# Attention's second heads scaled by ScalarE, dense products spread anew over its steps, one signal per silu

## The chip, the cores and the metric

The kernel runs on one core of a Trainium2 chip. The metric is device microseconds of one execution; runs are compared by their medians. Before the change the median of 3 runs is 1513.92 us (1513.66 to 1514.63). TensorE is called PE here, VectorE DVE, ScalarE ACT, SyncE SP and GpSimd POOL.

## The reference

Two blocks follow each other on a sequence of 512 tokens of width 1024. Only part of the first block is touched. Its mixer has an SSM half and an attention half, each gated by a silu, and ends in a product with `w_out`:

```python
y_ssm = s5_mixer(ssm_u, ...) * jax.nn.silu(ssm_z)
y_attn = dsa_mixer(q, k, v, q_idx, k_idx, w_idx, ...) * jax.nn.silu(attn_z)
y = jnp.concatenate([y_ssm, y_attn], axis=-1) @ w_out[l]
# inside dsa_mixer, 8 heads of 64, per query the 128 best keys:
logits = jnp.where((dist >= 0)[:, :, None, :], logits + bias, -jnp.inf)
p = jax.nn.softmax(logits, axis=-1)
out = jnp.einsum('bqhk,bqkhd->bqhd', p, v_sel)
```

`ssm_z` and `attn_z` are columns of the dense product `h @ w_in`.

## The kernel before, in words

All fp32 products are made of three reduced-precision ones: each operand is split into a high and a low part (`w_hi`/`w_lo`, `h_hi`/`h_lo`), the high part by ACT (a CAST), the low part by DVE (a subtraction). The weights stream by SP's queue through three slots of `w_raw`.

The program of each engine is written out by hand and runs in that order; engines wait for each other by counting semaphores (`wait_ge`, `then_inc`). In the attention of the first block the 512 queries are 4 tiles of 128 and the 8 heads are 4 pairs, which gives **16 steps** j. Step j handles heads i = 2j and 2j+1 (a *pair*), of query tile j // 4; its probabilities are 128 x 128 (steps 0 to 3), 128 x 256, 128 x 384 or 128 x 512 (steps 12 to 15). The pair's buffers alternate between `sgb` and `sqb`.

- **PE** (loop L975): logits of pair j+1 (L942), transposes of pair j, one head after the other (L954), values of pair j-1 (`values`, into `bank[7]`), then `GATE_UNITS[j]` *units* of dense work. A unit (`gemm_unit`, L618) is one k-tile of the products for `attn_z` and `ssm_z`: three matmuls over 512 columns. Eight units make a *half* (128 output columns); the first of eight halves runs ahead of the loop, seven halves, 56 units, lie in the steps. Then values 15 and the product with `w_out` (`out1`, L985), whose first k-tiles need the SSM tiles and whose fifth needs the last attention tile.
- **DVE** (loop L2400): in step j it waits for both exponentials of the pair, takes the reciprocals of the row sums (L2404) and scales both heads by them (L2406), each scaling counted in `p_norm`; then it masks the logits of pair j+1 (`masked_logits`, L2345 and L2349). Behind that stand low parts of weights (`GATE_LOW`), rounds of the key selection, and the gatings (`attn_gated`, `ssm_gated`), which wait for the silus by `az_ready`.
- **ACT** (loop L1620): in step j the exponentials of pair j+1 (L1560), between them the copies of the transposed pair j out of PSUM (`turned_copy`, L1569, the copy into `pT` waits for the values two heads before). Then what the step's tables name: `gate_half` copies a finished half out of its bank (`GATE_DONE`), `gate_high` is half a CAST of the next weights (`GATE_HIGH`), `attn_high` and `ssm_high` are high parts of gated tiles. After step 7 come the four silus of `az`, after step 14 three of `sz`, after step 15 the fourth. A silu after an exponential, and an exponential after a silu, makes ACT load a table.

Semaphore counts tie these together: a transpose waits for `p_norm` of its head, a mask for the transposes of the pair before last (their buffer is the same), the first unit of a half for the evacuation of its bank.

Of the kernel before, what the change touches and what calls it, by code (L numbers as in the profile page):

```python
# [164 lines left out]
def hybrid_blocks(nc, wstream, xT, vecs, consts, head_rows, onehot, rel_bias, ssm_vec, ssm_b, ssm_c, d_skip,  # L165
                  alpha2, decay, reset, outT):
    f32, f32r, i32 = mybir.dt.float32, mybir.dt.float32r, mybir.dt.int32
    ALU, ACT, AX = mybir.AluOpType, mybir.ActivationFunctionType, mybir.AxisListType
# [10 lines left out]
    with ctx:  # L179
# [14 lines left out]
        def sem(name):  # L194
            return ctx.enter_context(nc.semaphore(name))
# [114 lines left out]
        az_ready = sem("az_ready")  # L310
# [11 lines left out]
        copied_act, copied_dve = sem("copied_act"), sem("copied_dve")  # L322
        rel_psum, relu_ready, rel_used = sem("rel_psum"), sem("relu_ready"), sem("rel_used")
        lg_psum, lg_ready, p_exp, p_norm = sem("lg_psum"), sem("lg_ready"), sem("p_exp"), sem("p_norm")
        lg_read, pt_psum, pt_ready, pv_psum, pv_read = sem("lg_read"), sem("pt_psum"), sem("pt_ready"), sem("pv_psum"), sem("pv_read")
        gain_high, gain_low = sem("gain_high"), sem("gain_low")
        x_reload, x1_done, x1_stored, x1_back = sem("x_reload"), sem("x1_done"), sem("x1_stored"), sem("x1_back")
# [125 lines left out]
        def prob(i, qt):  # L453

            return (sgb, sqb)[i // 2 % 2][:, i % 2, 0:P * (qt + 1)]
# [3 lines left out]
        for name, n in (("glu", 4), ("merge2", 8), ("ret_g", 8), ("merge0", 8), ("gla_g", 8),  # L459
# [7 lines left out]
        GATE_HIGH = {2: (2, 0), 3: (2, 1), 6: (3, 0), 7: (3, 1), 11: (4, 0), 12: (4, 1)}  # L467
        GATE_LOW = {0: ((1, 0), (1, 1)), 1: ((1, 2), (1, 3)), 4: ((2, 0), (2, 1)), 5: ((2, 2), (2, 3)),
                    8: ((3, 0), (3, 1)), 9: ((3, 2), (3, 3)), 13: ((4, 0), (4, 1)), 14: ((4, 2), (4, 3))}
        GATE_UNITS = [4] * 8 + [3] * 8  # L470
        GATE_DONE = {0: 0, 2: 1, 4: 2, 6: 3, 8: 4, 11: 5, 14: 6, 15: 7}
        RET_FILL = [(gr, half) for name in ("ret_q", "ret_k", "ret_v") for gr in G[name] for half in range(2)]
        MERGE_FILL = {n: [(gr, half) for gr in G[f"merge{n}"] for half in range(2)] for n in (0, 2)}

# [98 lines left out]
        def _(pe):  # L573
# [168 lines left out]
            for i in range(8):  # L742
                ada_groups("ada_shift_scale", i, silu_w, bank[4 + i // 2][:, i % 2 * WC:i % 2 * WC + WC])
                if i == 2:
                    pe.wait_ge(rstd_ready, 1)
                    for t in range(TT):
                        ins = mm(stat_bank("norm0")[:, t * P:t * P + P], ones[:, :], rstd[:, t * P:t * P + P],
                                 True, True)
# [5 lines left out]
                if i == 0:  # L754
                    pe.wait_ge(presum_ready, 1)
                    for t in range(TT):
                        ins = mm(stat_bank("norm0")[:, t:t + 1], rstd[:, t * P:t * P + P], ones[:, 0:1], True, True)
# [7 lines left out]
            for k in range(KT):  # L765
# [4 lines left out]
                ins = mm(out, wl[:, k, :], h_hi[:, k, :], False, k == KT - 1)  # L770
# [4 lines left out]
            for t in range(TT):  # L775
                ins = pe.transpose(bank[3][:, t * HEADS:(t + 1) * HEADS], sqb[64:64 + HEADS, 0, t * P:t * P + P],
                                   ident[64:64 + HEADS, 64:64 + HEADS])
# [6 lines left out]
            for b in range(8):  # L784
# [3 lines left out]
                for i in range(4):  # L788
                    ins = pe.transpose(bank[5 + b % 2][:, i * P:i * P + P], src[:, 4 * (b % 4) + i, :], ident)
# [45 lines left out]
            for w, gr in enumerate(G["q"]):  # L835
                for half in range(2):
                    n = 2 * w + half
                    for k in range(KT):
                        gemm_unit(gr, half, k, h_hi, h_lo)
                        if k % 2:  # L840
                            i = 8 * n + k + 3
# [9 lines left out]
            for half in range(2):  # L851
                for w, bk in ((win_re, 4 + half), (win_im, 6 + half)):
                    for j in range(8 * half, 8 * half + 8):
                        for gp in range(2):
                            ins = mm(bank[bk][gp * 64:gp * 64 + 64, (j % 8) * CHUNKS:(j % 8 + 1) * CHUNKS],
                                     w[:, j, gp * 64:gp * 64 + 64], ut[:, 2 * j + gp, :], True, True)
# [47 lines left out]
            for q in range(4):  # L904
                pe.wait_ge(k_ready, q + 1)
                for i in range(4):
                    j = 4 * q + i
# [5 lines left out]
                    for r in range(2):  # L913
                        ins = mm(outs[r], ut[:, 2 * j + r, :], toep[:, 2 * j + r, :], False, True)
# [3 lines left out]
            for b in range(4):  # L918
                if b % 2 == 0:
                    pe.wait_ge(y_act, b + 2)  # L920
                for t in range(4):
                    ins = pe.transpose(bank[4 + b][:, t * P:t * P + P],
                                       u[:, b % 2 * 4 + t, b // 2 * P:b // 2 * P + P], ident)
# [21 lines left out]
            def transposes(j):  # L945

                qt = j // 4
                for r in range(2):
                    i = 2 * j + r
                    pe.wait_ge(p_norm, i + 1)  # L950
                    if j:
                        pe.wait_ge(pt_ready, i - 1)
                    for s in range(qt + 1):
                        ins = pe.transpose(bank[PT_BANKS[r]][:, s * P:s * P + P],  # L954
                                           prob(i, qt)[:, s * P:s * P + P], ident)
                    ins.then_inc(pt_psum, 1)
# [56 lines left out]

            def swa_transposes(n):

                pe.wait_ge(p_norm, 32 + n + 1)
                for kb in range(1 if swa_at(n)[1] == 0 else 2):
                    t = PT_END[n - 1] + kb if n else 32
                    if t >= 34:
                        pe.wait_ge(pt_ready, t - 1)  # L1020
                    for j in range(4):
                        ins = pe.transpose(bank[ST_BANKS[t % 2]][:, j * P:j * P + P],  # L1022
                                           lg[:, n % 2, j, kb * P:kb * P + P], ident)
                    ins.then_inc(pt_psum, 1)
# [130 lines left out]
            for h in range(4):  # L1155
# [25 lines left out]
                for e in range(2):  # L1181
                    for t in range(TT):
                        ins = pe.transpose(bank[GO_BANKS[e]][:, t * P:t * P + P], by_token[:, t, e * P:e * P + P], ident)
# [100 lines left out]
        def _(act):  # L1284
# [260 lines left out]
            for w, gr in enumerate(G["glu"]):  # L1545
                ahead(gr)
                for half in range(2):
                    m = 2 * w + half
# [7 lines left out]
            def probabilities(i):  # L1556
# [3 lines left out]
                act.activation(prob(i, qt), prob(i, qt), ACT.Exp, scale=-1.0,  # L1560
                               bias=stat[:, 1, i:i + 1], accum_out=stat[:, 2, i:i + 1]).then_inc(p_exp, 1)

            def turned_copy(i):

                qt, r = i // 8, i % 2
                act.wait_ge(pt_psum, i + 1)
                if i >= 2:
                    act.wait_ge(pv_psum, i - 1)
                act.copy(pT[:, r, 0:qt + 1, :],  # L1569
                         bank[PT_BANKS[r]][:, 0:P * (qt + 1)].rearrange("p (s c) -> p s c", c=P))\  # L1570
                   .then_inc(pt_ready, 1)
# [21 lines left out]
            def gate_silu(x, ms):  # L1593

                for m in ms:
                    ins = act.activation(x[:, m, :], x[:, m, :], ACT.Silu)
                ins.then_inc(az_ready, 1)

            def attn_kept(qt):

# [17 lines left out]
            probabilities(1)  # L1618
            ahead(GATE_TILES[0])
            for j in range(16):  # L1620
                for r in range(2):
                    if j + 1 < 16:
                        probabilities(2 * j + 2 + r)
                    turned_copy(2 * j + r)
                if j == 4 or j == 8:
                    attn_kept(j // 4 - 1)
                if j == 15:
                    ssm_high(0)
                    ssm_high(1)
                if j in GATE_DONE:  # L1630
                    gate_half(GATE_DONE[j])
                if j in GATE_HIGH:
                    gate_high(*GATE_HIGH[j])
                if j == 7:
                    gate_silu(az, range(4))
                if j == 9:
                    attn_high(0)
                    attn_high(1)
                if j == 12:
                    attn_high(2)  # L1640
                if j == 14:
                    gate_silu(sz, range(3))
# [279 lines left out]
        def _(dve):  # L1922
            steps = 0

            def settle(ins):

                nonlocal steps
                steps += 1
                ins.then_inc(dve_step, 1)
                dve.wait_ge(dve_step, steps)  # L1930
# [437 lines left out]
            def attn_gated(qt):  # L2368

                rows = slice(qt * P, qt * P + P)  # L2370
                dve.wait_ge(az_ready, 1)
                a = y_attn(qt)
                if qt < 2:
                    dve.wait_ge(pv_read, qt + 1)
                    out = q32[:, :, rows]
                else:
                    dve.wait_ge(pv_psum, 8 * qt + 8)
                    out = by_tile(bank[PV_BANK][:, :])
                dve.tensor_tensor(by_tile(new_val(a)), out, az[:, :, rows], ALU.mult).then_inc(act_val, 1)
                if qt >= 2:  # L2380
                    dve.wait_ge(act_val, a + 1)
                    dve.nop().then_inc(pv_read, 1)
# [5 lines left out]

            def ssm_gated(m):

                dve.wait_ge(az_ready, 2 + m // 3)
                dve.tensor_tensor(new_val(y_ssm(m)), z32[:, m, :], sz[:, m, :], ALU.mult).then_inc(act_val, 1)

            def ssm_low(m):
# [5 lines left out]
            for j in range(16):  # L2400
                i = 2 * j
                qt = i // 8
                dve.wait_ge(p_exp, i + 2)
                settle(dve.reciprocal(stat[:, 3, i:i + 2], stat[:, 2, i:i + 2]))  # L2404
                for r in range(2):
                    dve.tensor_scalar(prob(i + r, qt), prob(i + r, qt), stat[:, 3, i + r:i + r + 1], None,  # L2406
                                      ALU.mult).then_inc(p_norm, 1)
                if j + 1 < 16:
                    masked_logits(i + 2)
                    masked_logits(i + 3)  # L2410
                for part in GATE_LOW.get(j, ()):
                    gate_low(*part)
                if j in (2, 3, 6, 7):
                    select_keys(1)
                if j == 9:
                    attn_gated(0)
                    attn_gated(1)
                if j == 10:
                    attn_low(0)
                    attn_low(1)  # L2420
                if j == 12:
                    attn_gated(2)
                if j == 13:
                    attn_low(2)
# [521 lines left out]
```

## Time and profile before

| what | value |
|---|---|
| median of 3 runs | 1513.92 us (1513.66 to 1514.63) |
| the profiled execution | 1514.99 us, its span 1513.2 us |
| PE busy | 1480.8 us |
| DVE busy | 826.3 us |
| ACT busy | 606.3 us |
| the attention's 16 steps | about 240 to 319 us of the span |

The profile is of one execution. A busy PE means that a matmul is recorded in flight; their ends are modelled, and in a dense run each lasts about 0.39 us with the next one beginning 0.23 us after it. The timelines give each instruction's start from the span's beginning, and in brackets how long the engine was idle before it and what released it. ACT and DVE overlap the end of one instruction with the start of the next by about 0.1 us.

### The profile page before, as it was taken

Reading aid. Unit: us, or ns where it says so; the run is one execution under the profiler, and the core shown is the slowest. Engines: PE = TensorE matmul, PEld = TensorE weight load, DVE = VectorE, ACT = ScalarE, POOL = GpSimd, SP = SyncE. Lnnn points to the kernel's source line nnn. Section 1 sums busy time; section 2 is a strip of 40 time slices with the busy share of each in tenths; the row PEclk is TensorE's granted clock in tenths of the full one; section 3 lists DMA queues with packets and bytes.
Section 4 is the critical chain, followed back from the end, with each engine's and each line's share of the span. In section 5 each row is a group of like instructions: output and inputs, shape, how many; then the busy total and the mean of one; then the engine's idle time right before and its main releaser. Section 6 shows DMA issues by size and latency. Waiting matters only on the chain.

```text
span 1513.2 us, 19862 instructions
## 1 busy us (share of the span) xinstructions
PE 1480.8 (98%) x8112; PEld 1202.0 (79%) x8112; DVE 826.3 (55%) x1351; ACT 606.3 (40%) x924; POOL 22.1 (1%) x39
## 2 busy tenths in 40 slices
PE   7999999999999999999999999999999999999997
PEld 5766967677887887888889777888888888888887
DVE  6978978865647663334336343533449544443233
ACT  4356335663336553334346434432334323232221
POOL 0020100000000000000000000000000000000000
PEclk9999999999999999999999999999999999999998
DMA  8531542043321112222222212222331222232221
GB/s 338 191 112 57 115 156 97 29 168 139 111 76 65 57 57 67 73 84 84 94 109 84 84 56 84 84 86 110 139 111 60 108 86 110 84 112 77 104 98 56
DMA packets 25001, 151.69 MB, mean 100 GB/s; under 512 B 3568, under 2 KB 6240, under 8 KB 8896
## 3 DMA queue, kind: packets, MB, share of 16 engines
q1 hardware_dynamic: 22304, 136.71, 25.2%
q0 software_dynamic: 2608, 13.72, 3.3%
q8 instruction: 64, 1.05, 0.3%
q14 instruction: 25, 0.20, 0.0%
HBM read 143.83 MB, written 7.88 MB: 100 GB/s over the span
## 4 chain that ended last, share of the span: by engine, by line
PE 89%; DVE 6%; ACT 2%; issue 1%; DMA 1%; DVEq 0%; SPq 0%; ACTq 0%
PE bank L575 87%; DMA w_raw<-wstream 1%; PE bank L1022 1%; DVE tmp L1933 1%; DVE score L2243 1%; DVE w_lo L1980 0%; PE bank L954 0%; DVE win_im L1933 0%; DVE win_re L1933 0%; DVE y_lo L2006 0%; DVE h_lo L2006 0%; DVE tval L2480 0%; ACT w_hi L1305 0%; DVE score L2228 0%; DVE sgb L2345 0%
## 5 line engine op out<-in xcount | busy, mean ns | idle before, releaser
L575 PE MATMUL bank<-h_hi,w_hi 128*128 128x512 f32 (+1 forms) x1104 | 438.2, 397 | 2.6 <-DVE w_lo L1980 1.3
L575 PE MATMUL bank<-h_hi,w_lo 128*128 128x512 f32 (+1 forms) x1120 | 436.5, 390 | 0.0
L575 PE MATMUL bank<-h_lo,w_hi 128*128 128x512 f32 (+1 forms) x1104 | 428.9, 390 | 0.0
L1980 DVE TENSOR_TENSOR w_lo<-w_raw,w_hi 128x2048 fp32r<-128x2048 f32 (+2 forms) x104 | 234.5, 2255 | 248.9 <-ACT w_hi L1305 247.6
L1305 ACT CAST w_hi<-w_raw 128x2048 fp32r<-128x2048 f32 (+2 forms) x108 | 202.6, 1876 | 136.5 <-PE bank L575 130.1
L575 PEld LDWEIGHTS bank<-h_hi,w_hi 128*128 128x128 f32 (+1 forms) x1104 | 206.8, 187 | 59.1 <-issue 14.3
L575 PEld LDWEIGHTS bank<-h_hi,w_lo 128*128 128x128 f32 (+1 forms) x1120 | 209.8, 187 | 44.8
L575 PEld LDWEIGHTS bank<-h_lo,w_hi 128*128 128x128 f32 (+1 forms) x1104 | 207.0, 187 | 41.7 <-issue 0.2
L575 PE MATMUL bank<-y_hi,w_hi 128*128 128x512 f32 x272 | 108.9, 400 | 1.9 <-DVE y_lo L2006 1.9
L575 PE MATMUL bank<-y_hi,w_lo 128*128 128x512 f32 x272 | 106.1, 390 | 0.0
L575 PE MATMUL bank<-y_lo,w_hi 128*128 128x512 f32 x272 | 105.9, 389 | 0.0
L575 PE MATMUL bank<-w_hi,h_hi 128*128 128x256 f32 x352 | 101.3, 288 | 0.0
L575 PE MATMUL bank<-w_lo,h_hi 128*128 128x256 f32 x352 | 99.5, 283 | 0.0
L575 PE MATMUL bank<-w_hi,h_lo 128*128 128x256 f32 x352 | 99.5, 283 | 0.0
L1675 ACT ACTIVATE sgb<-bank 128x512 f32<-128x512 f32 x40 | 23.9, 598 | 151.1 <-PE bank L575 151.1
L575 PE MATMUL bank<-f_hi,w_lo 128*128 128x512 f32 (+1 forms) x220 | 76.2, 347 | 0.0
L575 PEld LDWEIGHTS bank<-w_hi,h_hi 128*128 128x128 f32 x352 | 67.4, 191 | 6.2 <-issue 6.1
L575 PE MATMUL bank<-f_hi,w_hi 128*128 128x512 f32 (+1 forms) x196 | 69.8, 356 | 0.0
L575 PE MATMUL bank<-f_lo,w_hi 128*128 128x512 f32 (+1 forms) x196 | 69.4, 354 | 0.0
L575 PEld LDWEIGHTS bank<-w_lo,h_hi 128*128 128x128 f32 x352 | 67.5, 192 | 0.0
L575 PEld LDWEIGHTS bank<-w_hi,h_lo 128*128 128x128 f32 x352 | 67.4, 192 | 0.0
L575 PEld LDWEIGHTS bank<-y_hi,w_hi 128*128 128x128 f32 x272 | 51.0, 188 | 16.3 <-DVE y_lo L2006 3.6
(407 smaller groups left out, 1820.0 us busy)
## 6 DMA issues: line engine op xcount, KB each, us to landing
w_raw<-wstream SPq DMA_DIRECT2D x119, 1024.0 KB, 4.8
w_raw<-wstream SPq DMA_DIRECT2D x4, 768.0 KB, 4.2
bias_rows<-bias_table POOLq DMA_DIRECT2D x1, 2560.0 KB, 11.4
xr<-xT SPq DMA_DIRECT2D x4, 512.0 KB, 4.9
bias<-bias_rows POOLq DMA_DIRECT2D x1, 2048.0 KB, 12.6
xr<-xT SPq DMA_DIRECT2D x1, 2048.0 KB, 8.5
x_saved<-xr POOLq DMA_DIRECT2D x1, 2048.0 KB, 11.1
xr<-x_saved POOLq DMA_DIRECT2D x1, 2048.0 KB, 8.2
```

The source lines that it names most:

```text
L575: return pe.matmul(out, lhsT, rhs, start=start, stop=stop)
L1022: ins = pe.transpose(bank[ST_BANKS[t % 2]][:, j * P:j * P + P], lg[:, n % 2, j, kb * P:kb * P + P], ident)
L1305: act.copy(hi_of(s)[:, 0:kt, :], w_raw[:, i % RAW_SLOTS, 0:kt, :]).then_inc(w_high, 1)
L1675: act.activation(sgb[:, m % 2, :], bank[bk][:, :], func).then_inc(bank_free[bk], 1)
L1933: settle(dve.tensor_tensor(out, a, b, op))
L1980: dve.tensor_tensor(w_low_of(s)[:, 0:kt, :], w_raw[:, i % RAW_SLOTS, 0:kt, :], hi_of(s)[:, 0:kt, :].bitcast(f32), ALU.subtract).then_inc(w ...
L2243: dve.scalar_tensor_tensor(out=score[:, qt, 0:w], in0=sgb[:, i % 2, 0:w], scalar=wi[:, qt, h:h + 1], in1=score[:, qt, 0:w], op0=ALU.mult, ...
```

## The change

Three edits, all in the first block's attention.

1. **Scaling.** DVE takes the pair's reciprocals, signals them (`recip_ready`) and scales only the first head. ACT scales the second head in place (`normed`: an Identity with the reciprocal as per-row factor, signalled by `p_norm_act`). ACT does this at the start of step j, before the exponentials of pair j+1; for pair 8 it does it at the end of step 7, before the silus of `az`. PE's transposes wait for `p_norm` (first head) and `p_norm_act` (second head).
2. **Units.** The 24 units of steps 8 to 15 go from 3 each to 6, 2, 3, 2, 2, 2, 4, 3. Half 5's copy out of its bank moves from step 11 to step 10.
3. **Silus.** Each silu counts in `az_ready`; the waits follow (4 for the attention's gatings, 5 + m for the SSM's).

```diff
--- before.py
+++ after.py
@@ -322,6 +322,7 @@
         copied_act, copied_dve = sem("copied_act"), sem("copied_dve")
         rel_psum, relu_ready, rel_used = sem("rel_psum"), sem("relu_ready"), sem("rel_used")
         lg_psum, lg_ready, p_exp, p_norm = sem("lg_psum"), sem("lg_ready"), sem("p_exp"), sem("p_norm")
+        recip_ready, p_norm_act = sem("recip_ready"), sem("p_norm_act")
         lg_read, pt_psum, pt_ready, pv_psum, pv_read = sem("lg_read"), sem("pt_psum"), sem("pt_ready"), sem("pv_psum"), sem("pv_read")
         gain_high, gain_low = sem("gain_high"), sem("gain_low")
         x_reload, x1_done, x1_stored, x1_back = sem("x_reload"), sem("x1_done"), sem("x1_stored"), sem("x1_back")
@@ -467,8 +468,8 @@
         GATE_HIGH = {2: (2, 0), 3: (2, 1), 6: (3, 0), 7: (3, 1), 11: (4, 0), 12: (4, 1)}
         GATE_LOW = {0: ((1, 0), (1, 1)), 1: ((1, 2), (1, 3)), 4: ((2, 0), (2, 1)), 5: ((2, 2), (2, 3)),
                     8: ((3, 0), (3, 1)), 9: ((3, 2), (3, 3)), 13: ((4, 0), (4, 1)), 14: ((4, 2), (4, 3))}
-        GATE_UNITS = [4] * 8 + [3] * 8
-        GATE_DONE = {0: 0, 2: 1, 4: 2, 6: 3, 8: 4, 11: 5, 14: 6, 15: 7}
+        GATE_UNITS = [4] * 8 + [6, 2, 3, 2, 2, 2, 4, 3]
+        GATE_DONE = {0: 0, 2: 1, 4: 2, 6: 3, 8: 4, 10: 5, 14: 6, 15: 7}
         RET_FILL = [(gr, half) for name in ("ret_q", "ret_k", "ret_v") for gr in G[name] for half in range(2)]
         MERGE_FILL = {n: [(gr, half) for gr in G[f"merge{n}"] for half in range(2)] for n in (0, 2)}
 
@@ -947,7 +948,7 @@
                 qt = j // 4
                 for r in range(2):
                     i = 2 * j + r
-                    pe.wait_ge(p_norm, i + 1)
+                    pe.wait_ge((p_norm, p_norm_act)[r], j + 1)
                     if j:
                         pe.wait_ge(pt_ready, i - 1)
                     for s in range(qt + 1):
@@ -1013,7 +1014,7 @@
 
             def swa_transposes(n):
 
-                pe.wait_ge(p_norm, 32 + n + 1)
+                pe.wait_ge(p_norm, 16 + n + 1)
                 for kb in range(1 if swa_at(n)[1] == 0 else 2):
                     t = PT_END[n - 1] + kb if n else 32
                     if t >= 34:
@@ -1560,6 +1561,12 @@
                 act.activation(prob(i, qt), prob(i, qt), ACT.Exp, scale=-1.0,
                                bias=stat[:, 1, i:i + 1], accum_out=stat[:, 2, i:i + 1]).then_inc(p_exp, 1)
 
+            def normed(i):
+
+                s = prob(i, i // 8)
+                act.wait_ge(recip_ready, i // 2 + 1)
+                act.activation(s, s, ACT.Identity, scale=stat[:, 3, i:i + 1]).then_inc(p_norm_act, 1)
+
             def turned_copy(i):
 
                 qt, r = i // 8, i % 2
@@ -1593,8 +1600,7 @@
             def gate_silu(x, ms):
 
                 for m in ms:
-                    ins = act.activation(x[:, m, :], x[:, m, :], ACT.Silu)
-                ins.then_inc(az_ready, 1)
+                    act.activation(x[:, m, :], x[:, m, :], ACT.Silu).then_inc(az_ready, 1)
 
             def attn_kept(qt):
 
@@ -1618,6 +1624,8 @@
             probabilities(1)
             ahead(GATE_TILES[0])
             for j in range(16):
+                if j != 8:
+                    normed(2 * j + 1)
                 for r in range(2):
                     if j + 1 < 16:
                         probabilities(2 * j + 2 + r)
@@ -1632,6 +1640,7 @@
                 if j in GATE_HIGH:
                     gate_high(*GATE_HIGH[j])
                 if j == 7:
+                    normed(17)
                     gate_silu(az, range(4))
                 if j == 9:
                     attn_high(0)
@@ -2368,7 +2377,7 @@
             def attn_gated(qt):
 
                 rows = slice(qt * P, qt * P + P)
-                dve.wait_ge(az_ready, 1)
+                dve.wait_ge(az_ready, 4)
                 a = y_attn(qt)
                 if qt < 2:
                     dve.wait_ge(pv_read, qt + 1)
@@ -2388,7 +2397,7 @@
 
             def ssm_gated(m):
 
-                dve.wait_ge(az_ready, 2 + m // 3)
+                dve.wait_ge(az_ready, 5 + m)
                 dve.tensor_tensor(new_val(y_ssm(m)), z32[:, m, :], sz[:, m, :], ALU.mult).then_inc(act_val, 1)
 
             def ssm_low(m):
@@ -2401,10 +2410,9 @@
                 i = 2 * j
                 qt = i // 8
                 dve.wait_ge(p_exp, i + 2)
-                settle(dve.reciprocal(stat[:, 3, i:i + 2], stat[:, 2, i:i + 2]))
-                for r in range(2):
-                    dve.tensor_scalar(prob(i + r, qt), prob(i + r, qt), stat[:, 3, i + r:i + r + 1], None,
-                                      ALU.mult).then_inc(p_norm, 1)
+                dve.reciprocal(stat[:, 3, i:i + 2], stat[:, 2, i:i + 2]).then_inc(recip_ready, 1)
+                dve.wait_ge(recip_ready, j + 1)
+                dve.tensor_scalar(prob(i, qt), prob(i, qt), stat[:, 3, i:i + 1], None, ALU.mult).then_inc(p_norm, 1)
                 if j + 1 < 16:
                     masked_logits(i + 2)
                     masked_logits(i + 3)
```

## Rows read from the trace of the kernel before

**Rows 1.** The page's first part: busy time of TensorE, share of the span, instructions.
```profile
PE 1480.8 (98%) x8112; PEld 1202.0 (79%) x8112; DVE 826.3 (55%) x1351; ACT 606.3 (40%) x924; POOL 22.1 (1%) x39
```
**Rows 2.** Windows (stretch and length in us, busy per engine, PEclk, DMA share, GB/s).
```profile
240.30:276.00 35.70, 35.70 (x194) 24.30 (x193) 28.97 (x93) 20.07 (x59) 0.00 (x0) 1.00 0.17 60
276.00:282.60 6.60, 4.59 (x30) 2.96 (x28) 4.32 (x12) 6.56 (x13) 0.00 (x0) 1.00 0.00 0
323.40:345.00 21.60, 21.60 (x95) 17.91 (x96) 10.62 (x12) 9.48 (x12) 0.56 (x1) 1.00 0.33 105
```
**Rows 3.** PE's timeline (start, us, operation, idle before and its releaser), steps 0 to out1.
```profile
240.30 0.44 PE L954 MATMUL bank<-cst,sgb 128*128 128x128 f32 x2
...
282.59 0.88 PE L954 MATMUL bank<-cst,sqb 128*128 128x128 f32 x6 [2.01 <-DVE sqb L2406]
...
288.12 0.88 PE L954 MATMUL bank<-cst,sgb 128*128 128x128 f32 x6 [0.71 <-DVE sgb L2406]
...
294.69 0.50 PE L575 MATMUL bank<-h_hi,w_hi 128*128 128x512 f32 x1
...
296.98 1.13 PE L575 MATMUL bank<-k,q 64*128 64x512 f32 x4
...
298.04 1.09 PE L954 MATMUL bank<-cst,sgb 128*128 128x128 f32 x8
...
313.64 1.09 PE L954 MATMUL bank<-cst,sqb 128*128 128x128 f32 x8 [0.61 <-DVE sqb L2406]
...
314.67 1.09 PE L575 MATMUL bank<-pT,v 128*64 128x128 f32 x16
...
323.37 0.50 PE L575 MATMUL bank<-y_hi,w_hi 128*128 128x512 f32 x1 [0.70 <-DVE y_lo L2006]
```
**Rows 4.** Who waited for whom, PE, 234 to 324 us (total, times, longest).
```profile
PE bank L575 <- DVE y_lo L2006: 1.5, 3, 0.7
```
**Rows 5.** ACT's timeline, steps 0 to 14.
```profile
239.12 1.89 ACT L1305 CAST w_hi<-w_raw 128x2048 fp32r<-128x2048 f32 x1
...
275.40 1.28 ACT L1596 ACT_TABLE_LOAD   x1
...
282.62 0.60 ACT L1590 COPY sz<-bank 128x512 f32<-128x512 f32 x1
...
286.96 1.22 ACT L1609 CAST y_hi<-tval 128x512 fp32r<-128x512 f32 x2 [0.73 <-DVE tval L2379]
...
297.93 1.05 ACT L1581 CAST w_hi<-w_raw 128x1024 fp32r<-128x1024 f32 x1 [0.17 <-ACT sz L1590]
...
303.19 0.62 ACT L1609 CAST y_hi<-tval 128x512 fp32r<-128x512 f32 x1
...
313.69 1.28 ACT L1596 ACT_TABLE_LOAD   x1
...
314.99 1.67 ACT L1596 ACTIVATE sz<-sz 128x512 f32<-128x512 f32 x3
```
**Rows 6.** Groups by line and form, ACT, 234 to 370 us (busy us, mean ns).
```profile
L1653 ACT ACTIVATE g_hi<-xr,vec 128x512 fp32r<-128x512 f32 x8 | 5.8, 725 | 26.2 <-DVE xr L2456 26.2
L1569 ACT COPY pT<-bank 128x512 f32<-128x512 f32 x8 | 4.4, 568 | 0.0
```
**Rows 7.** DVE's timeline, pairs 8, 9 and 15 and the last gating.
```profile
271.09 0.62 DVE L2345 SCALAR_TENSOR_TENSOR sgb<-bank,stat,bias 128x384 f32<-128x384 f32 x1 [0.94 <-PE bank L575]
...
281.91 0.17 DVE L2404 RECIPROCAL stat<-stat 128x2 f32<-128x2 f32 x1 [2.17 <-ACT sqb L1560]
...
282.11 0.75 DVE L2406 TENSOR_SCALAR sqb<-sqb,stat 128x384 f32<-128x384 f32 x2
...
308.91 0.74 DVE L2345 SCALAR_TENSOR_TENSOR sqb<-bank,stat,bias 128x512 f32<-128x512 f32 x1
...
321.79 0.69 DVE L2379 TENSOR_TENSOR tval<-bank,az 128x512 f32<-128x512 f32 x1
```
**Rows 8.** Span and mean granted clock of the core.
```profile
core 0: 1513.2 us, clock 0.997
```

## The prediction

> **What bounds the kernel now.** I read the page first: TensorE (PE) is busy for 1480.8 of 1513.2 us [rows 1], so there are some 32 us to win and only where PE stands still. The windows then show where that is: PE has no gap from 240.3 to 276.0 (steps 1 to 8 of the attention) and none from 323.4 to 345.0 (the out1 product), but only 4.59 busy of 6.60 us from 276.0 to 282.6 [rows 2]. PE's own timeline gives the waits inside the change's stretch: 2.01 us before pair 9's transposes, 0.71 before pair 10's, 0.61 before pair 15's [rows 3], and three at the start of out1, 1.5 us together, the last of which ends at 323.37 [rows 3, 4]. These 4.8 us, 0.32% of the time, are all that better filling can win. Everything else is what the change puts on ScalarE (ACT), so ACT's timeline is the third view [rows 5]: CASTs, table loads and silus are issued in program order, and whatever follows them waits.
>
> PE does the same dense work before and after (56 units in the steps), and after 323.4 nothing but PE sets the end. So the change in time is the change in PE's waits. I follow PE's **lag**: how much later it stands than before, with units done early credited. A unit is three products; 95 products take 21.60 us [rows 2], so a unit is 0.68 us.
>
> **The price of the new operation.** The second head is scaled by an ACT Identity in SBUF with a per-row factor. That operation with that kind of operand stands in the trace for 512 columns: 0.725 us; the plainest ACT pass over 512 columns, a copy, takes 0.568 [rows 6]. I take 0.72, 0.62 and 0.40 us for 512, 384 and 128 columns (the row itself, and less by some 0.1 per 128 columns), with 0.57 and 0.90 (a quarter more) as ends for 512. VectorE (DVE) gives up one of two scalings; two of 384 columns took 0.75 [rows 7], so 0.33 us goes at each such step, which counts only where DVE is last.
>
> **Term 1, step 0: +0.95.** ACT's program has a CAST of 1.89 us at 239.12 [rows 5] in front of the second head's scaling. It frees ACT at about 240.95; with 0.40 for 128 columns the head is ready at 241.4. Before, its transpose followed the first head's at 240.30 + 0.16 [rows 3]. PE has no gap in steps 1 to 8, so nothing gives the 0.95 back, and the softmax of pair 8 moves too: its first DVE row waits for PE [rows 7].
>
> **Term 2, steps 8 and 9: -0.30.** At step 7 the scaling of head 17 stands before the silus. Its reciprocal comes 0.95 later, and with its 0.62 the table load moves from 275.40 [rows 5] to 277.1, by 1.7; silus, the load back and pair 9's exponentials follow it. Pair 9's reciprocal moves from 281.91 [rows 7] to 283.6, its first transposes from 282.59 to 284.2. Its second head's scaling stands behind the gate copy of 282.62 [rows 5], so from 285.0 to 285.65; the transposes end at 286.05, against 283.39 before. PE has done three units more by then (six, not three): 2.66 - 2.04 leaves 0.62 to 0.65 lag.
>
> **Term 3, step 10: -0.44.** From one reciprocal to the next DVE was full for 5.54 us; without one scaling it takes 5.2, so pair 10's first head is ready at 289.4. The second waits on ACT for the two y_hi copies, which ended at 288.18 [rows 5] and move by 1.3; its scaling then ends at 290.05 and the transposes at 290.47, against 288.92. With two units in hand (1.36) lag is 0.2.
>
> **Term 4, steps 12 and 13: +1.85.** These steps had no wait before; now each has one unit less of cover, and a CAST of 1.05 us stands at the end of steps 11 and 12 [rows 5], ahead of heads 25 and 27. Step 12: PE arrives at 298.04 [rows 3] + 0.2 + 0.68 = 298.9. Logits 12 came 0.2 + 1.36 later, so the first head is ready at 299.2 (wait 0.27); the CAST, now without the gate copy before it, starts at 298.75, the scaling ends at 300.4 (wait 0.73 after the first head's 0.49 us). Step 13: head 24's copy waits for values 11, which end at 301.85; copy, exponential, copy, CAST and the y_hi copy of 0.62 [rows 5] are 3.1 us, the scaling 0.72: 305.7, where PE wants it at 304.9 (wait 0.85). Lag 2.05.
>
> **Term 5, step 15: +2.35, the largest.** Step 14 ends on ACT with a gate copy, a table load of 1.28 us and three silus of 1.67 [rows 5]; only step 7 has its scaling moved ahead of the silus, and head 31's comes behind these. Before, both heads of pair 15 were scaled by DVE at 313.6 while ACT did that, and PE waited 0.61 [rows 3]. Now logits 15 reach DVE at 310.05, where it began the pair at 308.91 [rows 7]: 1.14 later. So the silus end at 317.8, head 31 is scaled at 318.5, and its transposes end at 319.08, against 314.67 [rows 3]; the units done are equal (53). Between the two heads of one pair PE stands still for 3 us. Lag 4.4. What hid the scaling before was DVE's idleness: it had nothing else until 316.7.
>
> **Term 6, the start of out1: -0.95.** PE gets there late enough to find k-tiles 0 and 1 ready. Values 14 (1.02) and three units (2.29 [rows 3]) end at 322.4; the last gate copy and silu (0.7 and 0.62) at 323.9; two DVE operations later the last gating starts at 325.25, against 321.79 [rows 7]. From there to out1's last wait nothing changes: 323.37 becomes 326.85. The silus' own signals cost and win nothing: the first gated tile can start 1.1 us earlier, but its y_hi copy still stands on ACT behind the turned copies of heads 30 and 31, which wait for values 14. Gate half 5's evacuation one step earlier only moves 0.6 us on ACT, counted in term 4.
>
> **Sum:** 0.95 - 0.30 - 0.44 + 1.85 + 2.35 - 0.95 = 3.5 us. The profiled execution took 1514.99 us (its span 1513.2 and 1.8 around it); it would take 1518.5. The median of the runs is 1.07 lower, 1513.92, so I forecast 1517.4. The price enters at five places (terms 1, 2, twice 4, 5): at 0.57 the sum falls to 2.7, at 0.90 it rises to 4.4, which makes the forecast's own range 1516.6 to 1518.3.
>
> **Rivals.** What a measurement can tell from no change is 0.2%, 3.0 us.
> *Partly absorbed (0.22).* The 0.95 of step 0 is lost in the wait of step 9, or the scaling is as cheap as a copy: 2.5 us, 1516.4, within 0.2%. For it: step 9 had 2.01 us of slack; against it: pair 8's DVE row waits for PE, so the whole chain moves.
> *Filled and freed (0.06).* Steps 9 to 15 are paced by DVE, which loses 0.33 to 0.40 us a step, and the extra units at steps 8 and 14 cover what is left: the three waits of 3.3 us go, step 0 still costs 0.95, the tail stays: -2.4, 1511.5 (with step 0 free, 1510.6). It decides from the point where head 31 is scaled before PE reaches its transposes, at about 315.5. For it: DVE was last at all three waits [rows 3]; against it: ACT's silus end two microseconds after that.
> *The clock falls in the new wait (0.05).* The wait of 2.01 us left the granted clock at 1.00 [rows 2]; the one at step 15 would be about 3 us, longer than any here. The mean granted clock is 0.997 [rows 8], so all time at the lower level (1.2 of 2.4 GHz) cost this run at most 0.003 x 1513 = 4.5 us, which bounds the price: up to 1522, about 1520 if half. The Trainium skill ("TensorE: Matmul & The Clock Gate", Part 1) says that the array falls to 1.2 GHz after an idle stretch and must work before it returns; by that rule this is what a long enough wait brings, and no wait of this trace shows it.
> *It isn't a filler operation (0.01).* Were Identity not served beside Exp, each step would load tables twice, 1.28 us each: 16 x 2.57 = 41 us, 1555. Against it: the eight Identity rows of [rows 6] stand between squares with no load among them.
>
> **How the numbers follow.** The forecast has 0.66. Slower: 0.66 + 0.05 + 0.01 = 0.72; same 0.22; faster 0.06. The range takes in most of the absorbed case and the milder clock case: 1515.3 to 1519.7.
>
> **What would show it.** In the changed profile: a PE wait of about 3 us before pair 15's second transposes, ended by ACT's scaling line; one of about 1 us in step 0, released by the same line; 0.7 to 0.9 at steps 12 and 13; the first out1 product near 323.5 and its last wait ending near 327. If the scaling rows last 0.72 and ACT has them before the silus of step 14, or pair 15's second head does not wait, the forecast is wrong; if step 0's wait is there but logits 9 are not later, term 1 is.

## The result and the profile after

The changed kernel took 1521.39 us (median of five runs, 1520.70 to 1523.50), the kernel before 1514.41 beside it (1513.66 to 1514.63). The ratio is 1.0049, with a 95% interval of 1.0038 to 1.0060: slower by 7.0 us where 3.5 were forecast. The direction was right; the time lies 1.7 us above the stated range.

The profiled execution has a span of 1521.7 us against 1513.2 [rows 8], 8.5 more. The cores view, and the first part of the page:

```profile
core 0: 1521.7 us, clock 0.994
```
```profile
PE 1485.6 (98%) x8112; PEld 1205.1 (79%) x8112; DVE 821.8 (54%) x1335; ACT 614.0 (40%) x940; POOL 22.1 (1%) x39
```

The first thing to see stands against [rows 1]: PE runs the same 8112 matmuls, and yet is busy for 4.8 us more. Added waits can't do that. The granted clock is the place to look next (windows as in [rows 2]; the eighth value is PEclk):

```profile
284.00:287.20 3.20, 1.60 (x16) 1.11 (x16) 2.95 (x9) 2.66 (x8) 0.00 (x0) 1.00 0.00 0
287.20:290.60 3.40, 3.40 (x14) 2.04 (x10) 2.73 (x6) 2.70 (x7) 0.00 (x0) 0.50 0.00 0
318.00:321.35 3.35, 0.90 (x10) 0.73 (x12) 1.29 (x2) 2.39 (x5) 0.00 (x0) 1.00 1.01 435
321.35:324.75 3.40, 3.40 (x21) 2.70 (x16) 0.00 (x1) 1.63 (x4) 0.00 (x0) 0.50 0.80 333
444.25:447.60 3.35, 3.35 (x14) 2.64 (x13) 1.22 (x6) 2.06 (x10) 0.00 (x0) 0.50 0.38 161
```

Three stretches of 3.4 us ran at half clock: after step 9's waits, after step 15's, and once in unchanged program. In the trace of before the clock leaves 1.00 only in the last 10 us of the span, where PE has nearly nothing left to do:

```profile
1503.40:1513.10 9.70, 1.22 (x2) 0.50 (x2) 6.15 (x11) 0.00 (x0) 0.00 (x0) 0.50 0.32 108
```

Such a stretch at 0.50 is called a *fall* below; the one that ends every program is left out of the counts. PE's own timeline shows the waits, and what the clock does to the matmuls behind them (to be held against [rows 3]):

```profile
240.87 0.33 PE L955 MATMUL bank<-cst,sgb 128*128 128x128 f32 x1
241.90 0.33 PE L955 MATMUL bank<-cst,sgb 128*128 128x128 f32 x1 [0.69 <-ACT sgb L1568]
...
284.82 0.55 PE L955 MATMUL bank<-cst,sqb 128*128 128x128 f32 x3 [0.73 <-DVE sqb L2415]
286.24 0.55 PE L955 MATMUL bank<-cst,sqb 128*128 128x128 f32 x3 [0.87 <-ACT sqb L1568]
...
302.21 0.66 PE L955 MATMUL bank<-cst,sgb 128*128 128x128 f32 x4 [0.56 <-ACT sgb L1568]
...
307.67 0.66 PE L955 MATMUL bank<-cst,sqb 128*128 128x128 f32 x4 [0.77 <-ACT sqb L1568]
...
320.45 0.66 PE L955 MATMUL bank<-cst,sqb 128*128 128x128 f32 x4 [3.02 <-ACT sqb L1568]
321.04 1.72 PE L576 MATMUL bank<-pT,v 128*64 128x128 f32 x16
...
323.71 0.63 PE L576 MATMUL bank<-h_hi,w_lo 128*128 128x512 f32 x1
324.13 0.63 PE L576 MATMUL bank<-h_hi,w_hi 128*128 128x512 f32 x1
...
325.13 0.40 PE L576 MATMUL bank<-h_hi,w_hi 128*128 128x512 f32 x1
325.36 0.40 PE L576 MATMUL bank<-h_lo,w_hi 128*128 128x512 f32 x1
...
330.39 0.50 PE L576 MATMUL bank<-y_hi,w_hi 128*128 128x512 f32 x1 [0.70 <-DVE y_lo L2015]
```

Every wait that the forecast names as its sign is there, at its place and with its releaser: 0.69 in step 0, 0.56 and 0.77 in steps 12 and 13, 3.02 between the two heads of pair 15, all ended by ACT's scaling (L1568). 0.69 and 0.56 are shorter than forecast (about 1, and 0.7 to 0.9). Behind the 3.02 the values take 1.72 us, against 1.09 [rows 3], and the dense products start 0.42 us apart; from 325.13 on they start 0.23 apart again.

ACT's timeline shows what holds the scaling up, as the prediction worked it out: the CAST in step 0, the table load and three silus in step 14. The scaling has no table load of its own.

```profile
239.66 1.88 ACT L1306 CAST w_hi<-w_raw 128x2048 fp32r<-128x2048 f32 x1
241.44 0.40 ACT L1568 ACTIVATE sgb<-sgb,stat 128x128 f32<-128x128 f32 x1
...
277.00 0.61 ACT L1568 ACTIVATE sgb<-sgb,stat 128x384 f32<-128x384 f32 x1
...
316.82 1.28 ACT L1603 ACT_TABLE_LOAD   x1
318.12 1.67 ACT L1603 ACTIVATE sz<-sz 128x512 f32<-128x512 f32 x3
319.69 0.71 ACT L1568 ACTIVATE sqb<-sqb,stat 128x512 f32<-128x512 f32 x1
```

### The profile page after: what moved, and what is told of

Its sections match the earlier page's. It is cut to its first block, busy times and chain, and to the rows that moved or that the text cites. A ratio compares the mean times of both kernels' runs of the same rounds, so it can differ in the third digit from the quotient of the medians.

```text
span 1521.7 us, 19862 instructions
## 1 busy us (share of the span) xinstructions
PE 1485.6 (98%) x8112; PEld 1205.1 (79%) x8112; DVE 821.8 (54%) x1335; ACT 614.0 (40%) x940; POOL 22.1 (1%) x39
## 4 chain that ended last, share of the span: by engine, by line
PE 88%; DVE 6%; ACT 3%; DMA 2%; issue 1%; SPq 0%; DVEq 0%; ACTq 0%
PE bank L576 85%; DMA w_raw<-wstream 2%; PE bank L1023 1%; DVE w_lo L1989 1%; DVE tmp L1942 1%; DVE score L2252 0%; ACT w_hi L1306 0%; PE bank L955 0%; DVE score L2237 0%; DVE win_im L1942 0%; DVE win_re L1942 0%; DVE small L2236 0%; DVE h_lo L2015 0%; DVE tval L2488 0%; PE bank L1184 0%
```

## The experiments

The theory under test, A: the forecast's waits are real, the longer of them bring the granted clock down, and the rest of the 7 us is the clock. Its rivals put the whole loss on ACT's longer program and its waits, or on another part of the change, with the clock a bystander; what each expects of a run stands in the words put down before it. Each kernel was timed in five or more runs beside the kernel before: 1514.82 us median in the first set (the first four kernels below), 1514.94 in the second. The numbers in square brackets are the 95% interval of the ratio to before. One execution of each kernel was profiled, and two of the changed one. In these ten the first transposes of step 0 start anywhere from 239.47 to 242.36 us, since the stretch ahead of the change varies too: five of the ten have a fall at 18 to 20 us. A difference of 2 us between medians of five runs is therefore weak evidence, and what a wait or a fall costs is read from the traces, from step 0 on.

**The changed kernel again.** No edit; the base for the three that follow.

> The changed kernel once more, for the spread of its runs and a second profile. Theory A (waits of about 3.5 us plus falls of the clock, each worth 1.1 to 1.7 us): 1519 to 1523 us, with spans at 0.50 of the granted clock right behind the wait before pair 15's second transposes, and the number of such spans differing from run to run. Theory B (waits alone; what is above 3.5 us came from a late weight load at 234 us and from chance): 1517 to 1519 us, and the late load is not there again.

Measured: 1522.13 us (1520.74 to 1522.31), 1.0045 times before [1.0032, 1.0057]. Its trace has falls of 3.41 us at 285.7, 319.8 and 442.7, and one at 19.4. The first three come behind the same waits as above, so they are not one execution's accident; the one at 19.4 is ahead of all that the change touches.

**Work in the wait of step 15.** Eleven products into a bank that nothing uses then, between the two heads of pair 15; their sums are not used.

```
                     i = 2 * j + r
+                    if j == 15 and r == 1:
+                        pe.wait_ge(lg_read, 32)
+                        for _ in range(11):
+                            mm(bank[3][:, :], hi_of(GATE_TILES[3].s)[:, 0, 0:P], h_hi[:, 0, :], True, True)
```

> The changed kernel with eleven dense products of 512 columns (some 2.5 us, into a bank that is free, their result is not used) inside the 3.0 us wait before pair 15's second transposes; no wait gets shorter. Theory A (the clock falls because of that wait): no span at 0.50 behind step 15, 1.7 us less than the changed kernel beside it, about 1519.7. Theory B (waits alone): the same time as the changed kernel within 0.3 us.

Measured: 1519.98 us (1519.59 to 1524.48), 1.0041 [1.0027, 1.0054], its median 2.15 under the changed kernel's. PE's timeline of it:

```profile
316.52 0.60 PE L959 MATMUL bank<-cst,sqb 128*128 128x128 f32 x4
316.88 2.78 PE L576 MATMUL bank<-h_hi,w_hi 128*128 128x512 f32 x11
320.15 0.66 PE L959 MATMUL bank<-cst,sqb 128*128 128x128 f32 x4 [0.49 <-ACT sqb L1572]
320.73 1.09 PE L576 MATMUL bank<-pT,v 128*64 128x128 f32 x16
...
329.39 0.50 PE L576 MATMUL bank<-y_hi,w_hi 128*128 128x512 f32 x1 [0.70 <-DVE y_lo L2019]
```

The second head comes no sooner: 3.6 us behind the first, as before the edit. PE does useless work meanwhile, the clock stays at 1.00, and the values take 1.09 again. From there to out1's last wait it is 9.24 us (320.15 to 329.39), against 9.94 in the changed kernel (320.45 to 330.39) and 10.04 in its second profile. Were the clock a bystander, eleven useless products could win nothing; in the trace they win 0.7 to 0.8 us. The 2.15 us between the medians doesn't settle it: the two ratios' intervals nearly coincide, and while three of the five runs lie below all ten of the changed kernel, the other two, at 1522.24 and 1524.48, don't. The profiled one is that of 1522.24. It came to step 0 at 241.53, 0.7 us later than the first trace of the changed kernel and 2.0 later than the second, has a fall at 20.2 and one at 443.5, and none in the attention. It has none behind step 9 either, though it leaves those waits empty; what that gains is not the eleven products' doing.

**The same, and work in step 9's waits.** Three such products more ahead of each of pair 9's transposes.

```
+                    if j == 9:
+                        spare, half = GATE_HALVES[6]
+                        bk = pbanks(spare)[half]
+                        pe.wait_ge(bank_free[bk], uses(spare, half))
+                        for _ in range(3):
+                            mm(bank[bk][:, :], hi_of(GATE_TILES[2].s)[:, 0, 0:P], h_hi[:, 0, :], True, True)
```

> As the last one, and three such products ahead of each of pair 9's two transposes (0.7 us into waits of 0.73 and 0.87). Theory A: neither of the two falls inside the attention, 2.8 us less than the changed kernel, about 1518.6, which is before plus about 4. Theory B: the same time as the changed kernel, or up to 0.6 more from the products that don't fit the waits.

Measured: 1519.57 us (1518.55 to 1521.79), 1.0032 [1.0020, 1.0043]. In its profiled execution the clock never falls before the end of the program, which makes it the clean measure of the waits alone:

```profile
core 0: 1517.3 us, clock 0.997
```

That is 4.1 us over before's span, at before's clock. This execution came to the change 0.78 us earlier than before's, so the waits are worth some 4.8 us, and most of the rest of the 8.5 is the clock. Five of its six runs lie below all ten of the changed kernel.

**Head 31 ahead of the silus.** The scaling of head 31 is issued before step 14's silus, as head 17's is in step 7.

```
-                if j != 8:
+                if j not in (8, 15):
                     normed(2 * j + 1)
...
+                    normed(31)
                     gate_silu(sz, range(3))
```

> The changed kernel with ScalarE's scaling of head 31 ahead of the table load and the three silus of step 14, as head 17's is at step 7. Theory A: the 3.0 us wait goes and with it the fall behind it; the tail gives back some: 1.9 us of waits and 1.7 of clock, about 1517.8. Theory B: 1.9 us less alone. A third way, that the silus moved back by 0.72 cost as much at the start of out1: the same time.

Measured: 1519.06 us (1516.55 to 1521.18), 1.0023 [1.0010, 1.0036], 3.07 under the changed kernel. Its trace has no fall at step 15, and the second head follows the first after 0.8 us instead of 3.6:

```profile
316.01 0.60 PE L955 MATMUL bank<-cst,sqb 128*128 128x128 f32 x4
316.80 0.66 PE L955 MATMUL bank<-cst,sqb 128*128 128x128 f32 x4 [0.19 <-ACT sqb L1568]
```

Taking away the wait wins about 0.9 us more than only filling it (1519.98 to 1519.06). The intervals of the two ratios overlap, so that much is indicated, not settled. The traces point the same way: by the reckoning of the next section out1's last wait comes 3.76 us later than in before here, a fall behind step 9's waits included, and 4.79 in the trace of the filled wait, which has no fall there. Not all of the 2.8 us by which the head comes sooner reaches the end; one reason is told under term 6.

**The parts of the change one by one.** The change has three parts: units by need, silus that signal on their own, ACT's scaling. First the units and the silus without the scaling, DVE scaling both heads as before:

```
-                    pe.wait_ge((p_norm, p_norm_act)[r], j + 1)
+                    pe.wait_ge(p_norm, i + 1)
...
-                dve.tensor_scalar(prob(i, qt), prob(i, qt), stat[:, 3, i:i + 1], None, ALU.mult).then_inc(p_norm, 1)
+                for r in range(2):
+                    dve.tensor_scalar(prob(i + r, qt), prob(i + r, qt), stat[:, 3, i + r:i + r + 1], None,
+                                      ALU.mult).then_inc(p_norm, 1)
```

> The change without its first edit: VectorE scales both heads again, the units 6, 2, 3, 2, 2, 2, 4, 3 and the single silu signals stay. Theory A (all of the loss comes from the scaling on ScalarE and the clock falls that its waits bring): PE's waits by the steps' sums 0.6 us less than before (the 2.01 us wait of step 9 is filled, two of about 0.9 and 1.3 come at steps 14 and 10), no wait over 1.4: before minus 0.6, within 1 us of it. Rival C (the units are what costs, as they leave steps 9 and 11 to 13 uncovered): before plus 1.5 or more.

Measured: 1513.92 us (1513.00 to 1517.42), 0.9996 [0.9987, 1.0005]: no change. Its waits (PE, 234 to 334 us; total, times, longest) are 4.2 us, against some 4.8 before:

```profile
PE bank L955 <- DVE sgb L2413: 2.5, 3, 1.4
PE bank L576 <- DVE y_lo L2012: 1.5, 3, 0.7
PE bank L955 <- DVE sqb L2413: 0.2, 1, 0.2
```

The 2.01 us wait of step 9 is gone, and 1.41 of waiting at step 10 stands in its place.

Then ACT's scaling and the silus with the units of before, so that the waits of step 9 are filled by nothing:

```
-        GATE_UNITS = [4] * 8 + [6, 2, 3, 2, 2, 2, 4, 3]
-        GATE_DONE = {0: 0, 2: 1, 4: 2, 6: 3, 8: 4, 10: 5, 14: 6, 15: 7}
+        GATE_UNITS = [4] * 8 + [3] * 8
+        GATE_DONE = {0: 0, 2: 1, 4: 2, 6: 3, 8: 4, 11: 5, 14: 6, 15: 7}
```

> The change without its second edit: units 3 each in steps 8 to 15 as before, the scaling on ScalarE. Theory A: the wait of step 9 is back (2.6 us and 1.1 for the second head), the one at step 15 stays (3.3), so 5.7 us of waits over before, and at least two falls of the clock (3 us): before plus 8 to 9, slower than the whole change. Rival C (the units cost): faster than the whole change.

Measured: 1526.23 us (1525.89 to 1528.64), 1.0073 [1.0059, 1.0087]: the slowest of all. That is 11.3 us over before, where 8 to 9 were expected. Two rows of its timeline and two of its windows show the single wait of 2.78 us that has come in place of step 9's two, the wait of step 15 as it was, and falls of twice the length:

```profile
286.37 0.90 PE L955 MATMUL bank<-cst,sqb 128*128 128x128 f32 x3 [2.78 <-DVE sqb L2415]
...
324.71 1.12 PE L955 MATMUL bank<-cst,sqb 128*128 128x128 f32 x4 [3.02 <-ACT sqb L1568]
```
```profile
285.48:292.31 6.83, 5.43 (x23) 3.97 (x24) 5.78 (x14) 4.79 (x14) 0.00 (x0) 0.50 0.00 0
...
323.02:329.85 6.83, 5.14 (x25) 4.10 (x26) 1.43 (x3) 3.39 (x7) 0.00 (x0) 0.50 0.79 332
```

So the units by need are worth about 4 us where ACT scales (1526.23 to 1522.13; the lag at out1's last wait, reckoned as in the next section, is 9.99 against 6.45), and nothing that the runs can tell where DVE does. Without the scaling nothing is lost: the whole loss belongs to it.

The silus alone, with DVE's scaling and the units of before:

> The kernel before with the third edit alone: each silu signals by itself. Theory A: the first gated tile's multiply starts 1.1 us earlier but its high part still waits on ScalarE behind the turned copies of pair 15: the same time within 0.3 us. A rival that the signals are worth what they free: 1.1 us less.

Measured: 1515.06 us (1513.91 to 1516.77), 0.9999 [0.9990, 1.0007]: nothing, as argued. Its program is before's but for the signals, and yet its profiled execution had a fall of 3.41 us, at 437.4. It stands behind the two waits in unchanged program that are spoken of below.

**Units fitted to DVE's scaling.** The version that the others point to: DVE scales both heads, the silus signal on their own, and the 56 units are dealt out again, fewer in the early steps and more where PE waited.

```
-        GATE_UNITS = [4] * 8 + [6, 2, 3, 2, 2, 2, 4, 3]
+        GATE_UNITS = [3, 3, 3, 4, 3, 5, 3, 4, 6, 4, 2, 3, 2, 3, 5, 3]
```

> VectorE scales both heads; single silu signals; the 56 units spread as 3, 3, 3, 4, 3, 5, 3, 4, 6, 4, 2, 3, 2, 3, 5, 3, so that some of the first eight steps' units cover steps 9, 14 and 15. Theory A: the waits of steps 9, 10 and 15 go (3.3 us), those at the start of out1 shrink to two of 0.4 and 0.7: before minus 3.8 us, and no fall of the clock inside the attention. Rival C: no faster than before, since ScalarE's copies of finished halves now wait for PE in steps 2, 4 and 6 and delay the exponentials.

Measured: 1510.82 us (1510.34 to 1513.87), 0.9971 [0.9960, 0.9981]: 4.1 us faster than before, 11 faster than the change. Of the waits in the attention 0.2 us is left, and at out1 1.1:

```profile
PE bank L576 <- DVE y_lo L2012: 1.1, 2, 0.7
PE bank L576 <- DVE w_lo L1986: 0.2, 1, 0.2
PE bank L955 <- DVE sgb L2413: 0.2, 1, 0.2
```

Dealing the units out to the waits that a trace shows wins these 4 us; the change's own deal, with DVE scaling, won none of it, and against ACT's scaling it only made up for part of the waits that the scaling brings.

## Why the prediction fell short, term by term

The trace without falls (work in both waits) gives the lag of the waits alone. Three rows of PE's timeline from it:

```profile
240.58 0.33 PE L965 MATMUL bank<-cst,sgb 128*128 128x128 f32 x1 [0.74 <-ACT sgb L1578]
...
284.95 0.55 PE L965 MATMUL bank<-cst,sqb 128*128 128x128 f32 x3 [0.18 <-ACT sqb L1578]
...
318.14 0.66 PE L965 MATMUL bank<-cst,sqb 128*128 128x128 f32 x4 [0.48 <-ACT sqb L1578]
```

The *lag* of the prediction is read so: the start of a pair's second transposes, less its start in before, less the difference at step 0's first transposes (239.51 - 240.30, or -0.78 before rounding, for this trace came to the change earlier; +0.58 for the changed kernel's), less 0.68 for each unit done early. At step 15: 318.14 - 314.14 + 0.78 = 4.8 (314.14 is where head 31's four of the eight transposes begin in the merged row at 313.64 of [rows 3]).

```
                       forecast   waits alone   changed kernel
after step 0               0.95          0.90             0.86
after step 9               0.65          0.72             0.65
after step 10              0.2           0.36             1.40
after step 12              1.2           1.47             2.43
after step 13              2.05          2.44             3.39
after step 15              4.4           4.79             5.74
out1's last wait           3.5           4.78             6.45
```

**Terms 1 to 5 held.** As differences of the second column they are +0.90, -0.18, -0.36, +2.08 and +2.35, against +0.95, -0.30, -0.44, +1.85 and +2.35. The price of the scaling, taken from the row of another operand [rows 6], came out as taken: 0.40, 0.51, 0.61 and 0.72 us for 128 to 512 columns. The sizes of term 4 were a little low, 2.08 for 1.85. The rival of the table loads is dead, and so is "partly absorbed": step 9 gave nothing of step 0's 0.95 back, since the whole chain moved.

**Term 6 failed: 0.0 in place of -0.95.** I followed the chain from the last units over the gate copy and the silu to the last gating, with two DVE operations in between. The silu ends 4.73 us after head 31's transposes there (323.53 - 318.80), where 4.82 were forecast. But DVE does not take it up then. ACT, then DVE, from the same trace, and two rows of DVE from before:

```profile
320.19 1.08 ACT L1586 COPY pT<-bank 128x512 f32<-128x512 f32 x2 [2.10 <-PE bank L576]
321.15 1.15 ACT L1324 CAST y_hi<-tval 128x512 fp32r<-128x512 f32 x2
...
322.90 0.63 ACT L1613 ACTIVATE sz<-sz 128x512 f32<-128x512 f32 x1
```
```profile
321.81 0.69 DVE L2025 TENSOR_TENSOR y_lo<-tval,y_hi 128x512 fp32r<-128x512 f32 x1 [4.05 <-ACT y_hi L1324]
...
324.36 0.69 DVE L2411 TENSOR_TENSOR tval<-z,sz 128x512 f32<-128x512 f32 x1 [0.46 <-DVE y_lo L2025]
...
325.79 0.69 DVE L2398 TENSOR_TENSOR tval<-bank,az 128x512 f32<-128x512 f32 x1
```
```profile
318.17 0.69 DVE L2006 TENSOR_TENSOR y_lo<-tval,y_hi 128x512 fp32r<-128x512 f32 x1 [0.18 <-ACT y_hi L1313]
...
320.36 0.69 DVE L2392 TENSOR_TENSOR tval<-z,sz 128x512 f32<-128x512 f32 x1
```

The turned copies of heads 30 and 31 wait 2.10 us for values 14 on PE; the first y_hi copies stand behind them, and DVE, idle for 4.05 us, can begin its row of y_lo and gating only at 321.81. When the silu ends at 323.53 DVE is in the middle of that row, which keeps it until 323.90; then it is idle for 0.46 us and begins the silu's gating at 324.36, 0.83 us after the silu's end. The prediction names this order on ACT, but only as the reason why the silus' signals win nothing. In before the same turned copies stood behind the silus of [rows 5]. The row of y_lo and gating begins 3.67 us after head 31's transposes here (321.81 - 318.14) and 4.03 in before, so 0.36 us was given back up to there. But its first y_lo and the silu's gating are 2.55 us apart here and 2.19 in before (320.36 - 318.17): the idle 0.46 us, 0.10 in before, takes the 0.36 away again. The releaser shown, DVE's own y_lo, ends where the idle time begins, and nothing else that the gating waits for comes later, so the cause of it stays open; with head 31 ahead of the silus the same 0.46 us stands there. From head 31's transposes to out1's last wait it is 9.23 us in before (314.14 to 323.37) and 9.23 here (318.14 to 327.37): in all, no lag is given back. With head 31 ahead of the silus it is 9.99 (316.80 to 326.79): the copies again stand behind the silus, which end no sooner for it. That is where the gain of that edit goes in part.

**The clock: the step that failed most.** I held it a rival at 0.05, because the one wait of 2.01 us in before had left the clock at 1.00, and put it at nothing in the sum: "the change in time is the change in PE's waits", as if a product cost the same in every stretch. For step 15 the experiments show that the wait brings the fall: the three profiled executions with an empty wait of 3.02 us have one there, the three in which it is filled or gone have none, and with the wait filled the program behind it was 0.7 to 0.8 us shorter though the next head came no sooner. For step 9 that is not shown: three executions fell behind its two waits, but the one with work in step 15 alone left them empty and did not, and filling them too moved the median by 0.41 us only, inside the spread. What the falls cost in the profiled execution, from the last two columns: step 9's is worth 1.04 us at step 10 (1.40 - 0.36), some 0.96 of it still there at step 15, and with step 15's it is 1.67 at out1. The second fall adds only 0.7. The values take 0.63 longer (1.72 less 1.09), which goes straight into the chain just told; the dense products behind them lose some 0.9 more (three starts some 0.42 apart instead of 0.23, those at either end of the fall less so), but run beside that chain, for which out1 waits in any case. The rival's 1520 to 1522 holds the measured 1521.39, but that is in part luck. Its price was taken from the time that before's clock had lost, and the window above shows all of that at the end of the program, where it says nothing of a wait in step 15. The wait that the rival names cost 0.7 us; the rest came from term 6 and from two falls that it doesn't name. The Trainium skill ("TensorE: Matmul & The Clock Gate", Part 1) says that the array drops to half clock after it has idled and is raised again after work; for step 15 that agrees, with 0.50 granted behind the 3.02 us wait and 1.00 again behind the dense products.

**The third fall** is in program that the change doesn't touch, behind two waits of 0.93 and 0.97 us that every kernel here shows at this place. In the changed kernel and in before:

```profile
442.34 0.72 PE L576 MATMUL bank<-sk,sq 64*128 64x128 f32 x8 [0.93 <-DVEq L2567]
444.03 1.08 PE L576 MATMUL bank<-sk,sq 64*128 64x128 f32 x8 [0.97 <-DVE lg L2579]
```
```profile
435.35 0.71 PE L575 MATMUL bank<-sk,sq 64*128 64x128 f32 x8 [0.93 <-DVEq L2559]
437.03 0.71 PE L575 MATMUL bank<-sk,sq 64*128 64x128 f32 x8 [0.97 <-DVE lg L2571]
```

It costs the profiled execution 1.57 us (the lag over before is 7.02 ahead of it and 8.58 behind). The full sum for that execution: 0.58 from its later start into step 0 (PE waits 0.86 us for a weight's low part at 234.79, where before has no wait), 4.78 of waits, 1.67 from two falls, 1.57 from the third, 8.6 against a measured 8.5. A fall at this place stands in six of the ten profiled executions, that of the silus alone among them, and not in those of before, of head 31 first, of the work in both waits, and of the units and silus.

**What stays open.** The length of a wait alone doesn't decide. One of 2.01 us brought no fall in before, two of about 0.73 and 0.87 with a few transposes between them did in three executions, and did not in one other, and the same 0.93 and 0.97 did so in some executions and not in others. With one profiled execution of each kernel, two of the changed one, how often each fall comes was not measured. Of the 7.0 us between the medians, about 4.8 are waits (1519.57 less 1514.82, whose runs may hold falls of their own), and the remaining 2.2 to 2.6 the clock. The two ratios' intervals, 1.0032 [1.0020, 1.0043] and 1.0045 [1.0032, 1.0057], overlap, so this split of the medians is indicated; that of the profiled execution is read off its trace. Against the forecast of 1517.4, the waits are 1.3 us more than its 3.5, 0.95 of that in term 6; the 2.2 left over is put down to the clock; and the kernel before was 0.5 slower beside the change than on its own (1514.41, not 1513.92).

## What to carry to other kernels

Where TensorE sets the time, price a new wait twice: by its own length, and by the slower matmuls behind it, and give the second a real chance wherever the change makes waits longer, or puts them closer together, than the trace of before has them. Before crediting a late start with finding its inputs ready, list every chain that ends in them, and look for one that starts at the very step that came late. An operation moved to an engine with a program of its own is late by whatever stands ahead of it in that program: here 0.72 us of scaling made a wait of 3 us, while its old engine stood idle.

## What the runs showed of the hardware

Falls of the granted clock lasted 3.41 or 6.83 us, at 0.50 each time, and one at the start of the slowest kernel's profiled execution 10.24. In them 512-column products started 0.42 us apart instead of 0.23. In the changed kernel's profiled execution a fall of 3.41 us cost the end 0.7 to 1.6 us, by what ran beside it. The eleven useless products took 2.78 us in a wait of 3.02 and the head behind them came 3.63 us after the one before, as without them (3.62), which makes them a cheap probe for the clock.
